# A 31-tap depthwise convolution by even and odd columns: three filters of 16, 15 and 16 taps over half the columns in place of one over all

## The reference, cut to what matters

```python
def conv_module(h, pw1_w, pw1_b, dw_w, dw_b, ln_g, ln_b, pw2_w, pw2_b):
    z = h @ pw1_w + pw1_b
    a, g = jnp.split(z, 2, axis=-1)
    u = a * jax.nn.sigmoid(g)
    u = dwconv(u, dw_w, dw_b)          # 31 taps, each channel by itself, padded by 15
    u = jax.nn.silu(layernorm(u, ln_g, ln_b))
    return u @ pw2_w + pw2_b
```

## Time and profile before

| | us |
|---|---|
| median of 3 runs | 1765.65 (1763.65 to 1765.76) |
| the profiled execution, its own time | 1767.38 |
| its span in the profile | 1765.6 |
| PE busy in it | 1692.4 |
| DVE busy | 946.4 |
| ACT busy | 671.6 |
| POOL busy | 204.9 |

### The profile page before, as it was taken

The page is one execution under the profiler, slowest core; times in us unless marked ns, Lnnn a source line. Parts: engine busy times, 40 slices in busy tenths (PEclk is TensorE's granted clock), DMA queues, the critical chain, the costliest instruction groups (busy, mean ns, idle before and its releaser), DMA issues.

```text
span 1765.6 us, 25017 instructions
## 1 busy us (share of the span) xinstructions
PE 1692.4 (96%) x9946; PEld 1456.0 (82%) x9946; DVE 946.4 (54%) x1376; ACT 671.6 (38%) x967; POOL 204.9 (12%) x123
## 2 busy tenths in 40 slices
PE   6889886999999999999999999999999999999998
PEld 4666664899888888888899898989988988888887
DVE  3899997674433433234338544454535754443445
ACT  2556555653332323223245231313124533332334
POOL 1199994000000000000000000000000000000000
PEclk8899998999999999999999999999999999999999
DMA  8656663212122122222222222121212234323321
GB/s 296 203 186 225 197 231 126 72 53 77 41 82 72 48 71 62 63 66 59 60 61 63 60 54 72 49 54 53 73 49 84 61 98 116 96 83 108 95 84 48
DMA packets 240846, 165.63 MB, mean 94 GB/s; under 512 B 5289, under 2 KB 217113, under 8 KB 240761
## 3 DMA queue, kind: packets, MB, share of 16 engines
q1 hardware_dynamic: 237192, 151.48, 28.4%
q0 software_dynamic: 2704, 9.83, 1.7%
q10 hardware_dynamic: 864, 3.15, 0.5%
HBM read 162.34 MB, written 2.10 MB: 93 GB/s over the span
## 4 chain that ended last, share of the span: by engine, by line
PE 79%; POOL 11%; DVE 5%; ACT 2%; issue 1%; DMA 1%; SPq 0%; POOLq 0%; ACTq 0%; DVEq 0%
PE ps L490 78%; POOL conv L470 10%; DVE H_lo L1306 1%; POOL conv L473 1%; DVE w_lo L1265 1%; DVE rstd L1271 1%; DVE tmp L1294 1%; DVE sq L1294 1%; DMA tmp<-in_ffn_dw_w 0%; DVE rstd L1282 0%; DVE X L1463 0%; SPq L357 0%; DMA w_raw<-in_conv_pw_w 0%; ACT tmp L1050 0%; PE ps L792 0%
## 5 line engine op out<-in xcount | busy, mean ns | idle before, releaser
L490 PE MATMUL ps<-H_hi,w_hi 128*128 128x256 f32 (+1 forms) x1728 | 593.5, 343 | 26.3 <-DVE sq L1414 12.0
L490 PE MATMUL ps<-H_lo,w_hi 128*128 128x256 f32 (+1 forms) x1728 | 586.9, 340 | 0.0
L490 PE MATMUL ps<-H_hi,w_lo 128*128 128x256 f32 (+1 forms) x1728 | 586.2, 339 | 0.0
L490 PEld LDWEIGHTS ps<-H_hi,w_hi 128*128 128x128 f32 x1728 | 332.5, 192 | 79.3 <-issue 31.3
L1265 DVE TENSOR_TENSOR w_lo<-w_raw,w_hi 128x1024 fp32r<-128x1024 f32 x208 | 262.3, 1278 | 197.3 <-ACT w_hi L898 164.0
L490 PEld LDWEIGHTS ps<-H_lo,w_hi 128*128 128x128 f32 x1728 | 333.1, 193 | 34.6
L490 PEld LDWEIGHTS ps<-H_hi,w_lo 128*128 128x128 f32 x1728 | 332.4, 192 | 34.9
L490 PE MATMUL ps<-mid_hi,w_hi 128*128 128x512 f32 (+1 forms) x592 | 200.6, 339 | 0.5
L490 PE MATMUL ps<-mid_lo,w_hi 128*128 128x512 f32 (+1 forms) x592 | 199.5, 337 | 0.0
L490 PE MATMUL ps<-mid_hi,w_lo 128*128 128x512 f32 (+1 forms) x592 | 199.3, 337 | 0.0
L470 POOL TENSOR_TENSOR conv<-conv,prod 128x783 f32<-128x783 f32 x88 | 177.5, 2017 | 60.1 <-ACT prod L1007 48.3
(11 more groups left out here) (179 smaller groups left out, 1943.4 us busy)
## 6 DMA issues: line engine op xcount, KB each, us to landing
w_raw<-in_ffn_w_in SPq DMA_DIRECT2D x88, 512.0 KB, 3.8
ada<-in_ada_w SPq DMA_DIRECT2D x40, 1024.0 KB, 6.1
w_raw<-in_ret_w_in SPq DMA_DIRECT2D x40, 512.0 KB, 3.9
w_raw<-in_ffn_w_out SPq DMA_DIRECT2D x32, 512.0 KB, 4.0
w_raw<-in_conv_pw_w SPq DMA_DIRECT2D x24, 512.0 KB, 8.7
w_raw<-in_ffn_w_out SPq DMA_DIRECT2D x16, 384.0 KB, 3.3
ada<-in_ada_w POOLq DMA_DIRECT2D x4, 1024.0 KB, 6.2
w_raw<-in_ret_w_out SPq DMA_DIRECT2D x8, 512.0 KB, 3.7
```

The source lines that it names most:

```text
L490: return nc.tensor.matmul(o, a, b, start=first, stop=last, skip_group_check=True)
```

## The change

Write Ev(m) for the sum over the 16 even taps w[2j] of the even columns u[2(m+j)], and Od(m) for the sum over the 15 odd taps w[2j+1] of the odd columns u[2(m+j)+1], plus the bias. The even output column 2m is Ev(m) + Od(m). A third filter, of 16 taps, runs over the sum of neighbouring columns u[2k+1] + u[2k+2] with the weights w[2j] + w[2j+1] (w[30] alone for the last) and twice the bias. Its result S(m) holds the odd output column and also Od(m) and Ev(m+1), so the odd output column 2m+1 is S(m) − Od(m) − Ev(m+1). Each filter runs over 392 or 393 columns instead of 783 (the padding is one column more, so that OUTW is 784 and HALF is 392): 47 half-wide taps in place of 31 full ones.

The shares of the engines, per block:

- **DVE**: the gate products write the row in two planes, odd and even columns, 409 apart, their output stepping from plane to plane with each element. New: one TENSOR_TENSOR of 407 columns (`both_phases`, the sum of neighbours, both inputs in SBUF) and a wait for it. Then 16 taps of the sum filter (`sum_acc`, PSUM bank 3, the last into `tap_sum`), and 12 of the 16 even taps (`even_acc`, bank 4, the last into `tap_even`), by turns, so that each waits for the one before the last; the last four taps of the sum filter stand alone. 28 half-wide taps and one half-wide addition in place of 19 full taps.
- **ACT**: 15 odd taps and the last 4 even taps, 19 half-wide products in place of 12 full ones. The first two go straight to `odd_row` and `even_row`. The products of block b wait for the end of block b−2 (conv_ready).
- **POOL**: 17 half-wide additions from the ring in place of 11 full ones, and then 4 half-wide steps in place of one full one: even_row + tap_even, even_row + odd_row into every second column of `conv`, odd_row + even_row shifted by one, tap_sum − odd_row into the other columns of `conv`. Each waits for the one before.
- Once, ahead of the loop, DVE adds the weights in pairs (128x120), doubles the bias (128x8), and clears the padding in 6 small memsets as before.

```diff
+PRODS = ODD_TAPS + ACT_EVEN          (15 + 4)
+DVE_STEPS = DVE_EVEN + EVEN_TAPS     (12 + 16)
...
 @block.gpsimd
             for b in range(KT):
-                row = conv[:, b, 0:OUTW]
-                for n in range(1, ACT_TAPS):
...
+                for n in range(2, PRODS):
+                    at = (PRODS - 2) * b + n - 2
+                    pool.wait_ge(prod_ready, PRODS * b + n + 1)
+                    if at:
+                        pool.wait_ge(prod_added, at)
+                    odd = n < ODD_TAPS + 1
+                    row = odd_row[:, p, 0:HALF] if odd else even_row[:, p, :]
+                    w = HALF if odd else HALF + 1
+                    nc.gpsimd.tensor_tensor(row, row, prod[:, at % PROD_RING, 0:w], ALU.add).then_inc(prod_added, 1)
+                pool.wait_ge(prod_added, (PRODS - 2) * (b + 1))
+                pool.wait_ge(even_ready, b + 1)
+                nc.gpsimd.tensor_tensor(even_row[:, p, :], even_row[:, p, :], tap_even[:, p, :], ALU.add) \
+                    .then_inc(row_step, 1)
+                pool.wait_ge(row_step, 3 * b + 1)
+                nc.gpsimd.tensor_tensor(conv_rows(b)[:, 0, :], even_row[:, p, 0:HALF], odd_row[:, p, 0:HALF], ALU.add) \
+                    .then_inc(row_step, 1)
+                pool.wait_ge(row_step, 3 * b + 2)
+                nc.gpsimd.tensor_tensor(odd_row[:, p, 0:HALF], odd_row[:, p, 0:HALF], even_row[:, p, 1:HALF + 1], ALU.add) \
+                    .then_inc(row_step, 1)
+                pool.wait_ge(row_step, 3 * b + 3)
                 pool.wait_ge(slot_read[1], S_PW1 // 2 + b + 1)
-                nc.gpsimd.tensor_tensor(row, row, tap_row[:, b % 2, 0:OUTW], ALU.add).then_inc(conv_ready, 1)
+                nc.gpsimd.tensor_tensor(conv_rows(b)[:, 1, :], tap_sum[:, p, :], odd_row[:, p, 0:HALF], ALU.subtract) \
+                    .then_inc(conv_ready, 1)
...
 @block.scalar
+            def products(b):
                 act.wait_ge(slot_read[0], S_PW1 // 2 + b + 1)
+                if b >= 2:
+                    act.wait_ge(conv_ready, b - 1)
+                for n in range(PRODS):
...
+                    if n == 0:
+                        a = A(dst, frm, ACT.Identity, scale=w, bias=par[:, DW_B + b:DW_B + b + 1])
+                    else:
+                        a = A(dst, frm, ACT.Copy, scale=w)
...
 @block.vector
-                v.scalar_tensor_tensor(upad[b % 2][:, PAD:PAD + LAT], bank(0, 0), bias, rstd[:, LATS], ALU.add, ALU.mult)
...
+                v.scalar_tensor_tensor(out_phases(PAD, LAT), in_phases(bank(0, 0)), bias, in_phases(rstd[:, LATS]),
+                                       ALU.add, ALU.mult)
...
+                v.tensor_tensor(both_phases[:], phases(b)[:, 0, 0:QW], phases(b)[:, 1, 0:QW], ALU.add).then_inc(both_ready, 1)
+                dve.wait_ge(both_ready, b + 1)
                 ada_sum(4 + 2 * b, 0, 4 + b)
-                taps(b, range(12))
+                taps(b, range(8))
                 ada_sum(5 + 2 * b, 1, b)
-                taps(b, range(12, DVE_TAPS))
+                taps(b, range(8, EVEN_TAPS))
...
+            def taps(b, js):
+                for j in js:
+                    sum_tap(b, j)
+                    if j < DVE_EVEN:
+                        even_tap(b, j)
```

More of the change, by code:

```diff
@@ L172, in backbone @@
                 ada_more = sb("ada_more", [P, 2, KT // 2, GROUP * P], F32, start)
-            prod = sb("prod", [P, PROD_RING, OUTW + 1], F32, ph)
-            tap_row = sb("tap_row", [P, 2, OUTW + 1], F32, ph)
+            prod = sb("prod", [P, PROD_RING, HALF + 1], F32, ph)
+            odd_row = sb("odd_row", [P, 2, HALF + 1], F32, ph)
+            even_row = sb("even_row", [P, 2, HALF + 1], F32, ph)
+            tap_even = sb("tap_even", [P, 2, HALF + 1], F32, ph)
+            tap_sum = sb("tap_sum", [P, 2, HALF], F32, ph)
+            both_phases = sb("both_phases", [P, QW], F32, ph)
+            sum_w = sb("sum_w", [P, EVEN_TAPS * KT], F32, ph)
         with ExitStack() as ph:
@@ L198, in backbone, with phases, odd_in, even_in @@
         upad = [flat_tmp[:, 0:PADW], flat_sq[:, 0:PADW]]
+        def phases(b):
+            return upad[b % 2].rearrange("p (f m) -> p f m", f=2)
+        def odd_in(b, k, n):
+            return upad[b % 2][:, k:k + n]
+        def even_in(b, k, n):
+            return upad[b % 2][:, PHASE + k:PHASE + k + n]
+        def conv_rows(b):
+            return conv[:, b, :].rearrange("p (m f) -> p f m", f=2)
         def ada_row(m):
@@ L1018, in _ @@
                 ada_copy(2 * b + 5)
-                products(b, range(ACT_TAPS))
+                products(b)
             ada_copy(20)
@@ L1376, in _ @@
             for b in upad:
-                for lo, hi in ((0, PAD), (PAD + LAT, CTX_PAD), (CTX_PAD + CTX, PADW)):
-                    o = v.memset(b[:, lo:hi], 0.0)
+                for lo, hi in ((0, PAD // 2), (PAD // 2 + LAT // 2, CTX_PAD // 2), (CTX_PAD // 2 + CTX // 2, PHASE + 1)):
+                    o = v.memset(b.rearrange("p (f m) -> p f m", f=2)[:, :, lo:hi], 0.0)
             o.then_inc(padded, 1)
[L1382 to L1401, removed]
@@ new lines, in _, with sum_done @@
+            pairs = par[:, DW_W:DW_W + 2 * ODD_TAPS * KT].rearrange("p (j f b) -> p j f b", f=2, b=KT)
+            v.tensor_tensor(sum_w[:, 0:ODD_TAPS * KT].rearrange("p (j b) -> p j b", b=KT), pairs[:, :, 0, :], pairs[:, :, 1, :],
+                            ALU.add).then_inc(sum_w_ready, 1)
+            v.tensor_scalar(sum_w[:, ODD_TAPS * KT:], par[:, DW_B:DW_B + KT], 2.0, None, ALU.mult).then_inc(sum_w_ready, 1)
+            def sum_done(b, j):
+                return (DVE_STEPS - 2) * b + (2 * j + 1 if j < DVE_EVEN else DVE_EVEN + j)
@@ new lines, in even_done, with sum_tap @@
+            def even_done(b, j):
+                return (DVE_STEPS - 2) * b + 2 * j + 2
+            def sum_tap(b, j):
+                frm = both_phases[:, j:j + HALF]
+                if j < ODD_TAPS:
+                    w = sum_w[:, KT * j + b:KT * j + b + 1]
+                else:
+                    w = par[:, DW_W + KT * 2 * j + b:DW_W + KT * 2 * j + b + 1]
+                if j:
+                    dve.wait_ge(tap_done, sum_done(b, j - 1))
+                if j == 0:
+                    v.tensor_scalar(sum_acc, frm, w, sum_w[:, ODD_TAPS * KT + b:ODD_TAPS * KT + b + 1],
+                                    ALU.mult, ALU.add).then_inc(tap_done, 1)
+                elif j < EVEN_TAPS - 1:
+                    v.scalar_tensor_tensor(sum_acc, frm, w, sum_acc, ALU.mult, ALU.add).then_inc(tap_done, 1)
+                else:
+                    if b >= 2:
+                        dve.wait_ge(conv_ready, b - 1)
+                    v.scalar_tensor_tensor(tap_sum[:, b % 2, :], frm, w, sum_acc, ALU.mult, ALU.add)                         .then_inc(slot_read[1], 1)
+                    dve.wait_ge(slot_read[1], S_PW1 // 2 + b + 1)
@@ new lines, in even_tap @@
+            def even_tap(b, j):
+                frm = even_in(b, j, HALF + 1)
+                w = par[:, DW_W + KT * 2 * j + b:DW_W + KT * 2 * j + b + 1]
+                if j:
+                    dve.wait_ge(tap_done, even_done(b, j - 1))
+                if j == 0:
+                    v.tensor_scalar(even_acc, frm, w, None, ALU.mult).then_inc(tap_done, 1)
+                elif j < DVE_EVEN - 1:
+                    v.scalar_tensor_tensor(even_acc, frm, w, even_acc, ALU.mult, ALU.add).then_inc(tap_done, 1)
+                else:
+                    if b >= 2:
+                        dve.wait_ge(conv_ready, b - 1)
+                    v.scalar_tensor_tensor(tap_even[:, b % 2, :], frm, w, even_acc, ALU.mult, ALU.add)                         .then_inc(even_ready, 1)
+                    dve.wait_ge(even_ready, b + 1)
```

60 lines of the change are left out of this document (38 added, 22 removed).

## The result

| | before | after |
|---|---|---|
| median, us | 1765.7 (1763.65 to 1766.55, 4 runs) | **1754.73** (1753.74 to 1758.2, 4 runs) |
| ratio, 95% interval | | 0.9943 (0.9926 to 0.996) |
| profiled execution, its own time | 1767.38 | 1754.34 |
| its span | 1765.6 | 1751.7 |

What follows compares the result with a forecast made beforehand. POOL and DVE were taken to be at the limit together, PE close behind. POOL's block of 26.7 against 25.7 us added 8 over eight blocks: 1767.4 + 8 − 0.3 = 1775, median 1.7 lower, so 1773; range 1758 to 1785.

Steps and rivals of the forecast that it cites:

- the duration of one addition: POOL's half-wide addition: 0.20 us fixed plus half of 1.686, so 1.043; bounds 0.944 and 1.143.
- my 26.7: POOL's block after the change, in us: 21.9 of additions, 2.8 of gaps, 2.0 of turns, against 25.7 before.
- The first rival: POOL's addition nearly proportional to width: 0.944 each, block 24.6, kernel 1757; chance 0.17 for faster.
- point of decision: First rival's threshold: with a POOL addition from 0.975 us downward the block falls below 25.2, so faster.
- The turns: POOL's additions and DVE's two-SBUF-input operations wait for each other: 1.62 us for low parts, 0.4 for `both_phases`, 2.0 per block.
- TensorE's loop: PE's work, sigmoids and gate products: 22.1 us per block, 24.6 with 2.5 more; would stop the first rival at 1757.
- the gaps: Between POOL's additions, each waiting for its predecessor: 20 x 0.14 = 2.8 us per block.
- the price of the fixed share: Part of a POOL addition independent of width: 0.20 us, taken from DVE; a rival with 0.40 gave 1789, chance 0.1.
- no starving of POOL: Between two blocks: the bridge to new products takes 7.0 us, while POOL still has 10.5 us of work.
- strided writes by POOL: Closing steps writing every second column: taken as free; the rival adds 2.1 us a block, 1790, chance 0.07.
- jumps between planes: DVE's gate products: 1.2 us per block, or 2.4 if jumps of 409 columns halve their rate.
- Taking turns between accumulators: DVE's half-wide taps: step 0.53 us instead of 0.66, so 15.4 per block, or 18.5 if it brings nothing.

Runs made afterwards that it cites:

- the aligned kernel: The changed kernel with ring, odd_row, even_row and tap_even padded to a pitch of 396 columns instead of 393: 1768.44 us, ratio 1.0017.
- the later runs: The changed kernel with every pair of POOL's addition inputs one or two words apart, 1744.17 us; then also 13 instead of 12 even taps on VectorE, 1739.61 us.
- the last run: The changed kernel with every pair of inputs apart, and 13 instead of 12 even taps on VectorE: 1739.61 us, ratio 0.9851.
- the run with 18 taps: The kernel before with POOL's inputs one word apart, and 18 instead of 19 taps on VectorE: 1758.68 us, ratio 0.996.

## Why the prediction was wrong

**The step that failed is the duration of one addition.** I took 0.20 us fixed and let the rest halve with the width, 1.043. Measured are two prices: 1.03 to 1.05 where the inputs lie 0 or 3 words apart, 0.88 to 0.89 where they lie 1 or 2 apart. The ring's 112 odd-tap additions averaged 0.955 us:

```profile
L505 POOL TENSOR_TENSOR odd_row<-odd_row,prod 128x392 f32<-128x392 f32 x112 | 107.0, 955 | 64.0 <-ACT prod L1061 48.2 <-POOL odd_row L505 1.3
```

The difference to the aligned kernel is 10.9 us of the stage, and about 14 of the whole. Of the 2.2 us per block that lie between my 26.7 and the measured 24.5 (195.9 / 8), this is 1.4; the turns and one closing step, below, are the rest. My sum scaled a duration by one thing that changed, the width, and not by the others: the diff also changed the pitch of the buffers, from 784 to 393 words. The trace of before could not have given the fast rate, since it held only one alignment. But the diff showed that the places would change.

**The first rival named the right size for the wrong reason.** It priced an addition at 0.944 and the block at 24.6, and its 1757 lies 2.3 us from the median, by proportionality. The additions are not proportional; a mean of two rates lies there by chance. The measured mean of 0.955 lies on the side of its point of decision, 0.975, that it named for faster.

**The turns were put too high.** I took 1.62 for the low parts and 0.4 for `both_phases`, 2.0 per block. In the aligned kernel the three even-tap additions take 1.522 instead of 1.04 each, 1.45 in sum, and L511 0.2 more than the 1.01 it takes in the last block, where the trace has it beside no turn: 1.65. Together with L514, the one closing step whose inputs lie one word apart (0.88), additions at 1.03 instead of 1.043, and gaps of 2.7 instead of 2.8, that is the way from my 26.7 to the 25.8 measured.

**TensorE's loop was put too long.** I held 24.6 us per block for the point where PE stops any gain: 22.1, and 2.5 for a block at the lower clock. The change itself already has blocks of 24.4, and the later runs have 22.9 and 22.4. The 22.1 held, the 2.5 did not. The 2.5 belonged to the kernel of before: there the granted clock was 0.54 behind a wait of 3.99 us, and 0.92 over the stage, in which PE was busy for 175.6 us. In the last run, with shorter blocks, PE waits at most 1.0 us for a gate product, the granted clock over the stage is 1.00, and nearly the same number of matmuls (1013, 1011 before) keeps PE busy for 164.7 us. The low clock went with PE's waiting, and went away with it, so it was no floor. The term did not touch the forecast, whose block was longer, but it entered the price of the first rival.

**Right**: the stage and its bound, 168 instructions, the gaps (about 0.14 each in the ring, less between closing steps; the aligned block holds 23.2 of POOL's time and 2.7 of gaps, where I had 2.8), the price of the fixed share, VectorE at the limit with POOL before and idle for 3 us after, no starving of POOL, no wait for `tap_even`, PE not the bound in the change. ScalarE's half-wide products follow each other at 0.53 us and not at my 0.48, at no cost, since ScalarE waits for POOL.

**The rivals**: strided writes by POOL cost nothing. The gate products did become slower by their jumps between planes, 1.09 and 0.63 against 0.74 and 0.47, and it cost nothing, because VectorE was no longer the limit. Taking turns between accumulators brought the step of 0.53 that I took. The rows of two taps in a row, and the low parts with their new wait:

```profile
155.15 0.63 DVE L1477 SCALAR_TENSOR_TENSOR ps<-sq,par,ps 128x393 f32<-128x393 f32 x1
155.68 0.62 DVE L1461 SCALAR_TENSOR_TENSOR ps<-both_phases,sum_w,ps 128x392 f32<-128x392 f32 x1
...
172.05 3.54 DVE L1320 TENSOR_TENSOR w_lo<-w_raw,w_hi 128x1024 fp32r<-128x1024 f32 x2 [2.86 <-ACT w_hi L944]
175.52 1.09 DVE L1508 SCALAR_TENSOR_TENSOR tmp<-ps,par,rstd 128x512 f32<-128x512 f32 x1
```

By the Trainium skill's figure (GPSIMD Engine Reference, section 3.1) I had estimated 0.27 us fixed and 1.08 for the half-wide addition. The measurement decides: 0.18 fixed, and 1.01 or 0.88 by itself. The Trainium skill's page gives one figure and names no dependence on the places; with 2.10 or 1.77 ns a column, 2048 columns would take 4.48 or 3.81 us, so its 4497 ns agrees with the aligned rate, carried on as an estimate from at most 783 columns.

## What to carry to other kernels

When a diff changes the shape of a buffer, price the places of the operands as well as their widths: on POOL a float32 addition whose second input begins one or two words behind the first within 16 bytes takes 1.77 ns a column instead of 2.10. In these kernels it was had by starting one operand a word later. Where two engines are at the limit together, neither half of a change shows its worth alone: measure the four combinations. Work taken from VectorE can come back as waiting, if its two-input instructions then begin in the middle of POOL's and meet more of them. And a loop of TensorE that ran at a low clock beside waits is no floor for a change that shortens them.

## What the runs showed of the hardware that I had not expected

- The two rates of POOL's addition by the distance of its inputs, with the order of the inputs counting (3 words behind is slow, 1 behind is fast), and the output's place not.
- The length of VectorE's pair of low parts, 3.2 to 5.1 us for the same work (5.14 in one block of the run with 18 taps), by how long POOL's additions are and where in one of them it begins.
- The granted clock over the stage rose from 0.92 to 1.00 as the blocks became shorter and TensorE waited less.
